# A two-layer attention trunk on one core: Q and K of four bodies as seven block products, with weight sums made by accumulating DMAs

## The chip, the core and the metric

One core of one Trainium2 chip. The metric is the device time of one execution in microseconds (us), the median of several runs. TensorE is called PE here, VectorE DVE, ScalarE ACT, GpSimd POOL and SyncE SP.

## The reference, cut to what matters

Two encoder layers over 256 tokens of width 2048, all in float32. Each layer normalizes x, multiplies it by one wide input matrix, sends slices of the result through several attention branches, gates them, multiplies by an output matrix, normalizes and adds to x.

```python
def odd_layer(x, pre_g, w_in, sink, w_out, post_g):
    h = rms_norm(x, pre_g)
    qc, kc, vc, gc, qd, kd, vd, gd = _split(h @ w_in, ODD_IN_WIDTHS)
    qc = partial_rope(qc..., pos)      # three groups of 8 heads, 128 wide
    kc = partial_rope(kc..., pos)
    oc = dilated_mixture_attention(qc, kc, vc...)   # (window, dilation) 128,1  512,4  2048,16
    ...
```

The second and third group of `dilated_mixture_attention` (dilations 4 and 16) are what the change touches: 16 heads, whose Q, K and V are 256 x 2048 times 2048 x 512 products, four heads at a time.

## The kernel before, in words

**Precision.** PE multiplies in float32r. Each weight and each activation is split into a high part (a copy rounded to float32r) and a low part (the rest), and each product is the sum of three: high x high, high x low, low x high.

**Weights.** They lie in memory as chunks of 128 x 2048 floats, 1 MB: four row blocks of 128 (a quarter of K = 2048) by 512 columns. SP loads chunk after chunk into four raw buffers (`raw`, L282), each once DVE has split what was there. ACT writes the high part of a chunk to `w_hi` (L639, `split_hi`), DVE the low part to `w_lo` (L899, `split_lo`), in three buffers each, two chunks ahead of PE. PE multiplies a chunk in two halves of 12 matmuls of 128x512 (L383, in `products`, called by `half_chunk`): 2 row blocks x 2 token tiles x 3 terms.

**Bodies.** A body is 12 chunks: four for a block of 512 columns of Q, four for K, four for V, each into its own pair of PSUM banks `acc[blk][t]`, one bank for a token tile. ACT takes a finished block out of PSUM with the norm's factor (`take`, L646) into `unit`. Layer 0 has five bodies, layer 1 eight. The first body of a layer has no attention beside it.

**Attention beside it.** While the products of body b run, the unit of body b - 1 is worked on: its Q and K are rotated by POOL (`rotate`, L334 to L341, four operations for each of Q and K), turned by PE (L463) and copied by DVE (L940), and each of four heads goes through scores (PE L481), mask and maximum (DVE L969, L980, L986), exponential (ACT L661), turning (PE L517, DVE L1024) and weighing of V (PE L529, DVE L1044). `Unit.at`, `fills` and `stages` give the half chunk (slot) at which each step stands in the order that all engines share: a body has 24 slots. At the last slot `close` merges a group's output into `mix` by its softmax weights (L1063 to L1089). Units of kind G (dilations 4 and 16) are worked on beside bodies 3 to 6 of layer 1. They turn Q and K into `postg` (`g_qT`, `g_kT`) and need no split parts, so `qT` and `kT` are idle in them. `loops` makes an instruction loop of two turns for each kind.

**Order.** Each engine runs its own instructions in the order of the text; semaphores join them. `chunk_used` counts chunks that PE is done with, `hi_ready` and `lo_ready` splits, `proj_ready` taken blocks, `roped` rotated ones. POOL issues a few DMAs, among them the two of L361 that bring x in layer 1's token order, and L364's.

## Time and profile before

| | |
|---|---|
| median of 3 runs | 1217.54 us (1216.47 to 1217.96) |
| profiled execution | 1216.43 us |
| its span | 1214.6 us |
| PE busy | 1196.7 us (99%) |
| DVE busy | 707.6 us (58%) |
| ACT busy | 562.9 us (46%) |
| POOL busy | 78.7 us (6%) |
| DMA, mean over the span | 219.90 MB, 181 GB/s |
| clock granted to PE | 0.997 |

Times of rows are microseconds from the start of the span unless ns is written. A row of a group gives the line, the engine, the operation, the tiles out<-in, the shapes and the count, then the busy time, the mean of one in ns, and the idle time of the engine just before them with what ended it. A row of the order in time gives start, duration, engine, line, operation, tiles, shapes and count, and in brackets the idle time before it.

### The profile page before, as it was taken

The page shows a single profiled execution, that of the slowest core. Times are in us where ns is not written, and L with a number is a line of the kernel's source. Part 1 is how long each engine was busy: PE and PEld are TensorE (multiplying, and loading weights), DVE is VectorE, ACT ScalarE, POOL GpSimd, SP SyncE. Part 2 cuts the span into 40 slices and gives each one's busy share as a digit, 9 for nine tenths or more (in the row PEclk, how much of TensorE's full clock was granted, in tenths as well). Part 3 has the DMA queues.
Part 4 walks back from the last instruction along what each step waited for, and adds up shares of the span by engine and source line. Part 5 has one row for each costly group of instructions (what it writes and reads, how often), then busy time and mean ns, then how long its engine had stood idle before and what let it go on. Part 6 is the DMA issues. An engine that isn't in the chain of part 4 may idle for free.

```text
span 1214.6 us, 15429 instructions
## 1 busy us (share of the span) xinstructions
PE 1196.7 (99%) x5756; PEld 1001.0 (82%) x5756; DVE 707.6 (58%) x848; ACT 562.9 (46%) x734; POOL 78.7 (6%) x129
## 2 busy tenths in 40 slices
PE   7999999999999999999999999999999999999997
PEld 5788888888888888788888888888888888888886
DVE  5375555566664955754545545565656546667554
ACT  5554343454555644564444444444344444445442
POOL 2500000300000000010000000001000001000000
PEclk9999999999999999999999999999999999999999
DMA  9995354544436454455453545454544555334541
GB/s 361 251 305 195 141 188 156 173 144 169 173 138 242 173 208 173 173 201 180 157 190 140 180 163 178 169 186 159 208 142 169 187 193 208 139 139 173 179 168 69
DMA packets 33436, 219.90 MB, mean 181 GB/s; under 512 B 4288, under 2 KB 4416, under 8 KB 7920
## 3 DMA queue, kind: packets, MB, share of 16 engines
q1 hardware_dynamic: 30672, 209.73, 48.1%
q0 software_dynamic: 1856, 7.38, 2.4%
q10 hardware_dynamic: 864, 2.18, 0.5%
q8 instruction: 31, 0.51, 0.2%
q14 instruction: 13, 0.11, 0.0%
HBM read 217.17 MB, written 2.10 MB: 181 GB/s over the span
## 4 chain that ended last, share of the span: by engine, by line
PE 95%; DMA 3%; DVE 1%; ACT 0%; SPq 0%; issue 0%; ACTq 0%; DVEq 0%
PE acc L383 85%; PE bank_x L533 2%; DMA probs<-x_nat 2%; PE bank_x L517 1%; PE bank_y L487 1%; DMA raw<-weights 1%; PE bank_x L463 1%; PE bank_y L463 1%; PE bank_y L481 1%; PE bank_x L529 1%; PE bank_y L502 0%; PE bank_x L502 0%; PE bank_x L420 0%; PE bank_y L420 0%; DVE w_lo L899 0%; ACT w_hi L639 0%
## 5 line engine op out<-in xcount | busy, mean ns | idle before, releaser
L383 PE MATMUL acc<-w_hi,act_hi 128*128 128x512 f32 x1560 | 620.7, 398 | 2.6 <-DVE w_lo L899 2.6
L383 PE MATMUL acc<-w_lo,act_hi 128*128 128x512 f32 x1560 | 609.6, 391 | 0.0
L899 DVE TENSOR_TENSOR w_lo<-raw,w_hi 128x2048 fp32r<-128x2048 f32 x195 | 448.0, 2298 | 209.0 <-ACT w_hi L639 208.8
L639 ACT ACTIVATE w_hi<-raw 128x2048 fp32r<-128x2048 f32 x195 | 373.6, 1916 | 241.2 <-PE acc L383 215.5
L383 PE MATMUL acc<-w_hi,act_lo 128*128 128x512 f32 x1560 | 418.6, 390 | 0.0
L383 PEld LDWEIGHTS acc<-w_hi,act_lo 128*128 128x128 f32 x1560 | 293.2, 188 | 62.5 <-DVE act_lo L908 0.6
L383 PEld LDWEIGHTS acc<-w_hi,act_hi 128*128 128x128 f32 x1560 | 293.6, 188 | 60.1 <-DVE w_lo L899 2.3
L383 PEld LDWEIGHTS acc<-w_lo,act_hi 128*128 128x128 f32 x1560 | 294.0, 188 | 56.5
L646 ACT ACTIVATE unit<-acc,pre_r 128x512 f32<-128x512 f32 x78 | 49.3, 684 | 114.9 <-PE acc L383 114.5
L661 ACT ACTIVATE probs<-scores,negm 128x256 f32<-128x256 f32 (+1 forms) x80 | 36.7, 459 | 127.6 <-DVE negm L986 102.3
L334 POOL TENSOR_TENSOR rope_c<-unit,cst 128x256 f32<-128x256 f32 (+1 forms) x19 | 15.1, 797 | 663.8 <-ACT unit L646 663.7
L1024 DVE COPY pT<-bank_x 128x512 f32<-128x512 f32 (+1 forms) x48 | 28.8, 600 | 48.6 <-PE bank_x L517 48.6
L1044 DVE TENSOR_SCALAR mix<-bank_x 128x256 f32 (+1 forms) x24 | 10.1, 422 | 48.1 <-PE bank_x L533 48.1
L533 PEld LDWEIGHTS bank_x<-unit,pT 128*128 128x128 f32 x256 | 33.5, 191 | 2.5
L533 PE MATMUL bank_x<-unit,pT 128*128 128x128 f32 x256 | 33.7, 274 | 0.0
L1044 DVE TENSOR_SCALAR unit_out<-bank_x 128x256 f32<-128x256 f32 x16 | 6.8, 424 | 44.4 <-PE bank_x L529 44.4
L517 PEld LDWEIGHTS bank_x<-ident,probs 128*128 128x128 f32 x160 | 20.4, 140 | 6.2
L517 PE MATMUL bank_x<-ident,probs 128*128 128x128 f32 x160 | 25.2, 272 | 0.0
L831 ACT ACTIVATE probs<-acc 128x512 f32<-128x512 f32 x16 | 9.5, 595 | 32.4 <-PE acc L383 32.4
L980 DVE TENSOR_REDUCE rmax<-scores 128x2 f32<-128x512 f32 (+1 forms) x40 | 23.2, 580 | 1.4
L1042 DVE TENSOR_TENSOR mix<-bank_x,subg 128x256 f32 x8 | 3.4, 424 | 28.6 <-ACT bank_x L712 28.6
L313 POOL DMA_DIRECT2D mix<-rpb x32 | 19.6, 683 | 0.0
(172 smaller groups left out, 619.4 us busy)
## 6 DMA issues: line engine op xcount, KB each, us to landing
raw<-weights SPq DMA_DIRECT2D x195, 1024.0 KB, 4.8
resid<-x_turned SPq DMA_DIRECT2D x8, 256.0 KB, 10.1
mix<-rpb POOLq DMA_DIRECT2D x32, 64.0 KB, 25.2
postg<-post_g POOLq DMA_DIRECT2D x2, 1024.0 KB, 24.1
resid<-x_perm POOLq DMA_DIRECT2D x2, 1024.0 KB, 8.3
out<-resid SPq DMA_DIRECT2D x8, 256.0 KB, 2.5
raw<-weights SPq DMA_DIRECT2D x2, 512.0 KB, 6.0
postg<-x_nat ACTq DMA_DIRECT2D x2, 512.0 KB, 9.6
```

The costliest lines, as they stand in the source:

```text
L313: pool.dma_start(bias_in[half * 64:half * 64 + 64, at:at + SEQ].rearrange("p (j k) -> p j k", j=ROWS), src).then_inc(bias_in_two[h // 2], 16)
L383: m = nc.tensor.matmul(tiles[t][:, :], a[:, kt, t * P:(t + 1) * P], w[:, buf, kk * NB:(kk + 1) * NB], start=(kt == 0 and a is act_hi and w ...
L463: m = nc.tensor.transpose(bank[f % 2][:, n * P:(n + 1) * P], unit[:, blk, t, h * HEAD:(h + 1) * HEAD], ident[:, :])
L517: m = nc.tensor.transpose(X[:, at:at + P], p[:, t * w + k * P:t * w + (k + 1) * P], ident[:, :])
L533: m = nc.tensor.matmul(X[:, t * P:(t + 1) * P], pT[:, k * SEQ + t * P:k * SEQ + (t + 1) * P], unit[:, 2, k, col:col + HEAD], start=(k == 0 ...
L639: nc.scalar.activation(w_hi[:, at % SPLIT, :], raw[:, at % RAW, :], ACT.Copy).then_inc(S["hi_ready"], 1)
L646: m = nc.scalar.activation(dst[:, t, :], acc[blk][t][:, :], ACT.Copy, scale=pre_r[:, t:t + 1])
L661: m = nc.scalar.activation(probs[:, j % 2, t * w:(t + 1) * w], scores[:, j % 2, t * w:(t + 1) * w], ACT.Exp, bias=negm[:, 2 * j + t:2 * j ...
L899: nc.vector.tensor_tensor(w_lo[:, at % SPLIT, :], raw[:, at % RAW, :], w_hi[:, at % SPLIT, :].bitcast(F32), ALU.subtract).then_inc(S["lo_r ...
L980: nc.vector.reduce_max(rmax[:, two], dst.rearrange("p (t n) -> p t n", t=NT), AX_X).then_inc(S["maxed"], 1)
L1024: nc.vector.tensor_copy(pT[:, 0:n], X[:, 0:n]).then_inc(S["pt_ready"], 1)
L1044: nc.vector.tensor_scalar(dst, src, 1.0, None, ALU.mult).then_inc(S["o_taken"], 1)
```

## The change

In bodies 3 to 6 of layer 1, Q and K are no longer computed as eight products of (a token tile) x (half of K) by (half of K) x (the columns of Q or of K). With A11, A12 (first token tile; first, second half of K), A21, A22 (second tile), W11, W21 (columns of Q; first, second half of K), W12, W22 (columns of K), there are seven products (after Strassen and Winograd). They are named by their weight operand: W11 with A11; W21 with A12; P = W11 + W12 with S1; Q = W11 + W12 + W22 (as the source names it: P's block plus the next) with S2; R = W22 + W12 with S3; T = the sum of all four with A22; W22 with S5. S1, S2, S3 and S5 are sums and differences of parts of A, made once, in layer 1's first body (`sums`), and split into high and low.

- The body's list is `FAST_OPS`: 18 operations, each one chunk of 128x2048. V has four with 24 matmuls; the other fourteen have 12 matmuls each, into one bank of 128 tokens. A V operation has two slots, the others one: 22 slots.
- The sums of weights are made in the raw buffers: POOL issues a DMA of a further chunk with `accum_op=ALU.add` onto the chunk that is there, once DVE has split it: eight per body, behind POOL's two rotations. SP issues ten plain loads per body, in a written order, with a fifth raw buffer (`spare`, in the idle halves of `qT` and `kT`).
- ACT and DVE split most chunks in halves (`fast_split`), with semaphores for halves, and PE waits for high and low parts of each half on their own.
- ACT takes two results, DVE combines the rest out of PSUM: five `scalar_tensor_tensor` of 128x512. K is ready before Q, and POOL rotates in that order.
- x of layer 1 is kept in memory (`x_kept`) as `resid` holds sums; it comes back after the last G rotation. The loops over G bodies are written out.

```diff
+FAST0, FAST = 3, 4
+FAST_OPS = (("W11", 0), ("W11", 1), ("V", 0), ("V", 1), ("P", 0), ("P", 1), ("W21", 0), ("W22", 0), ("W22", 1),
+            ("Q", 0), ("Q", 1), ("V", 2), ("R", 0), ("R", 1), ("W21", 1), ("T", 0), ("T", 1), ("V", 3))
+FAST_RAW = (0, 1, 2, 3, 0, 1, 4, 2, 3, 0, 1, 4, 2, 3, 4, 0, 1, 2)
+FAST_SLOTS = [(o, x) for o, (name, _) in enumerate(FAST_OPS) for x in ((0, 1) if name == "V" else (None,))]
...
 @block.sync
+            for k in range(FAST):
+                op, d = first_op(1, FAST0 + k), CHUNK0[1] + BODY * (FAST0 + k)
+                load(2, d + 6, op + 3)
+                load(3, d + 7, op + 4)
+                load(4, d + 10, op + 7)
+                load(4, d + 3, op + 12)
+                load(2, d + 11, op + 13)
+                d += BODY
+                if k < FAST - 1:
+                    load(3, d + 9, op + 14)
+                    load(4, d + 2, op + 15)
+                    load(0, d, op + 16)
+                    load(1, d + 1, op + 17)
+                    load(2, d + 8, op + 18)
...
 @block.gpsimd
                     for k, (blk, cols) in enumerate(turns):
                         pool.wait_ge(S["proj_ready"], PROJ0[layer] + 3 * u.body - 2 + k)
                         pool.wait_ge(S["roped"], CREDIT + 2 * (u.index - 2) + k)
                         rotate(u, k, blk, cols, HEAD // 2 if layer == 0 else HEAD)
+                    if u.kind == "G":
+                        op, d = first_op(1, u.body), CHUNK0[1] + BODY * u.body
+                        for o, chunk in ((4, 4), (5, 5), (9, 6), (10, 7), (12, 4), (13, 5), (15, 2), (16, 3)):
+                            r = FAST_RAW[o]
+                            before = max(n for n in range(o) if FAST_RAW[n] == r)
+                            pool.wait_ge(S["lo_ready"], op + before + 1)
+                            pool.dma_start(raw[:, r, :], weights[d + chunk], accum_op=ALU.add).then_inc(added[r], 16)
...
 @block.tensor
+            def fast_body(u):
+                for h, (o, part) in enumerate(FAST_SLOTS):
+                    attention(u, h)
+                    name, c = FAST_OPS[o]
+                    ...
+                    if o == 6:
+                        pe.wait_ge(S["n1_taken"], k + 1)
+                    if o == 7:
+                        pe.wait_ge(S["n5_taken"], k + 1)
+                    if o == 12:
+                        pe.wait_ge(S["n6_taken"], k + 1)
+                    if o == 15:
+                        pe.wait_ge(S["proj_ready"], proj + 1)
+                    for half in (0, 1) if part is None else (part,):
+                        ... # wait for this half's high part; per row block: high and low of A times it
+                        ... # wait for this half's low part; per row block: high of A times it
+                        m.then_inc(S["chunk_used" if half else "half_used"], 1)
...
 @block.scalar
+            def fast_split(u, h):
+                k, op = u.body - FAST0, first_op(1, u.body)
+                o, part = FAST_SLOTS[h]
+                n = o + 2
+                ... # n >= FAST_N: whole split of the next body's chunk 0 or 1
+                for half in (0, 1) if part is None else (part,):
+                    if half == 0:
+                        if FAST_OPS[n][0] in FAST_SUMS:
+                            act.wait_ge(added[FAST_RAW[n]], fast_sums(k, n))
+                        else:
+                            act.wait_ge(landed[FAST_RAW[n]], fast_landings(k, n))
+                    if half == 0 and n >= 3:
+                        act.wait_ge(S["half_used"], FAST_N * k + n - 2)
+                    else:
+                        act.wait_ge(S["chunk_used"], op + n - 2)
+                    nc.scalar.activation(w_hi[:, buf, half * 2 * NB:(half + 1) * 2 * NB], raw_part(FAST_RAW[n], half),
+                                         ACT.Copy).then_inc(S["hi_ready" if half else "hi_half"], 1)
...
 @block.vector, fast_body: at each slot, ahead of attention(u, h) and fast_split(u, h)
+                    if h == 8:
+                        dve.wait_ge(S["chunk_used"], op + 6)
+                        ...
+                        nc.vector.scalar_tensor_tensor(c22, sum_c[:, :], r[1], c21, ALU.mult, ALU.subtract).then_inc(
+                            S["n5_taken"], 1)
+                    if h == 13:  # c12 from sum_b, n6_taken
+                    if h == 14:  # c12 from sum_c
+                    if h == 17:  # c22 from sum_b, proj_ready (K)
+                    if h == 20:  # c21 from sum_b, proj_ready (Q)
+            def sums(s):  # layer 1's first body, slots 6 to 11: 8 sums, 4 low parts, 128x1024 each
```

## Rows read from the trace of the kernel before

**Rows 1.** The page: engines over the span, and the chain by engine and line.
```profile
PE 1196.7 (99%) x5756; PEld 1001.0 (82%) x5756; DVE 707.6 (58%) x848; ACT 562.9 (46%) x734; POOL 78.7 (6%) x129
PE 95%; DMA 3%; DVE 1%; ACT 0%; SPq 0%; issue 0%; ACTq 0%; DVEq 0%
```
**Rows 2.** The chain in order of time, around 800 us: start, us, what.
```profile
800.49 5.47 PE acc L383 x24
...
809.59 0.45 PE bank_y L481 x4
810.04 8.18 PE acc L383 x36
...
821.18 0.44 PE bank_x L529 x4
```
**Rows 3.** ACT in order of time: the take of V, once in each body.
```profile
722.42 1.27 ACT L646 ACTIVATE unit<-acc,pre_r 128x512 f32<-128x512 f32 x2 [3.52 <-PE acc L383]
794.21 1.27 ACT L646 ACTIVATE unit<-acc,pre_r 128x512 f32<-128x512 f32 x2 [3.42 <-PE acc L383]
865.96 1.27 ACT L646 ACTIVATE unit<-acc,pre_r 128x512 f32<-128x512 f32 x2 [3.42 <-PE acc L383]
937.72 1.27 ACT L646 ACTIVATE unit<-acc,pre_r 128x512 f32<-128x512 f32 x2 [3.42 <-PE acc L383]
1009.53 0.69 ACT L646 ACTIVATE unit<-acc,pre_r 128x512 f32<-128x512 f32 x1 [3.48 <-PE acc L383]
```
**Rows 4.** Busy time by stretch, about a body each: length, engines, clock, DMA share, GB/s.
```profile
791.00:863.00 72.00, 72.00 (x346) 60.20 (x346) 42.13 (x55) 30.09 (x35) 4.60 (x8) 1.00 0.48 175
863.00:935.00 72.00, 72.00 (x346) 60.20 (x346) 42.12 (x54) 30.09 (x35) 4.60 (x8) 1.00 0.51 178
```
**Rows 5.** DVE in order of time in a G body, and groups of the whole span.
```profile
786.37 2.28 DVE L899 TENSOR_TENSOR w_lo<-raw,w_hi 128x2048 fp32r<-128x2048 f32 x1
788.57 0.16 DVE L1063 TENSOR_TENSOR newneg<-cneg,negm 128x8 f32<-128x8 f32 x1
...
797.31 2.29 DVE L899 TENSOR_TENSOR w_lo<-raw,w_hi 128x2048 fp32r<-128x2048 f32 x1 [0.22 <-ACT w_hi L639]
...
L894 DVE TENSOR_TENSOR w_lo<-raw,w_hi 128x1024 fp32r<-128x1024 f32 x2 | 2.5, 1226 | 3.2 <-ACT w_hi L631 1.9 <-ACT w_hi L628 1.3
L940 DVE COPY postg<-bank_x 128x512 f32<-128x512 f32 x8 | 5.5, 692 | 12.1 <-PE bank_x L463 12.1
L1024 DVE COPY pT<-bank_x 128x256 f32<-128x256 f32 x16 | 6.8, 424 | 22.7 <-PE bank_x L517 22.7
```
**Rows 6.** ACT by groups: splits of a whole chunk and of a half.
```profile
L639 ACT ACTIVATE w_hi<-raw 128x2048 fp32r<-128x2048 f32 x195 | 373.6, 1916 | 241.2 <-PE acc L383 215.5 <-DMA raw<-weights 25.6
L628 ACT ACTIVATE w_hi<-raw 128x1024 fp32r<-128x1024 f32 x1 | 1.1, 1056 | 1.1 <-DMA raw<-weights 1.1
```
**Rows 7.** POOL and DVE in order of time, at two rotations.
```profile
534.23 0.73 POOL L334 TENSOR_TENSOR rope_c<-unit,cst 128x256 f32<-128x256 f32 x1 [161.87 <-ACT unit L646]
535.88 2.29 DVE L899 TENSOR_TENSOR w_lo<-raw,w_hi 128x2048 fp32r<-128x2048 f32 x1 [3.14 <-ACT w_hi L639]
535.88 2.89 POOL L341 TENSOR_TENSOR unit<-rope_c,rope_s 128x256 f32<-128x256 f32 x1
...
1010.06 2.28 DVE L899 TENSOR_TENSOR w_lo<-raw,w_hi 128x2048 fp32r<-128x2048 f32 x1
1010.87 1.79 POOL L334 TENSOR_TENSOR rope_c<-unit,cst 128x128 f32<-128x128 f32 x1 [21.31 <-ACT unit L646]
1012.91 2.36 POOL L337 TENSOR_TENSOR rope_s<-unit,cst 128x64 f32<-128x64 f32 x1
```
**Rows 8.** DMA: a stretch with its engines full; issues by line; one of POOL's alone.
```profile
800.00:804.00 4.00, 4.00 (x22) 3.36 (x21) 3.58 (x3) 1.57 (x1) 0.00 (x0) 1.00 0.98 406
raw<-weights SPq DMA_DIRECT2D x195, 1024.0 KB, 4.8
mix<-rpb POOLq DMA_DIRECT2D x32, 64.0 KB, 25.2
postg<-post_g POOLq DMA_DIRECT2D x2, 1024.0 KB, 24.1
resid<-x_perm POOLq DMA_DIRECT2D x2, 1024.0 KB, 8.3
L364 POOL DMA_DIRECT2D postg<-post_g x1 | 0.6, 591 | 0.0
DMA to landing us min/median/max: 6.8/6.8/6.8
```

More of the change, by code:

```diff
@@ L229, in build @@
         x_new = [sem(f"x_new{t}") for t in range(NT)]
-        landed = [sem(f"landed{i}") for i in range(RAW)]
+        landed = [sem(f"landed{i}") for i in range(RAW + 1)]
+        added = [sem(f"added{i}") for i in range(RAW)]
         bias_in_two = [sem(f"bias_in_two{i}") for i in range(UH)]
@@ L244, in loops @@
                     yield Unit(kind, lay, body, index, 0, mask), body, 0
+                elif kind == "G" or eng is nc.gpsimd and lay == 1:
+                    for i in range(count):
+                        yield Unit(kind, lay, body, index, i, mask), body, i
                 else:
@@ L275, in _, with ring @@
                 load_x(2 * c + 1)
-            with sp.Fori(1, ALL_CHUNKS // RAW) as n:
-                src = [sp.snap(n * RAW + r) for r in range(RAW)]
-                free = [sp.snap(n * RAW + r - RAW + 1) for r in range(RAW)]
-                for r in range(RAW):
-                    sp.wait_ge(S["lo_ready"], free[r])
-                    sp.dma_start(raw[:, r, :], weights[bass.ds(src[r], 1)].rearrange("a p n -> p (a n)")).then_inc(
-                        landed[r], 16)
+            def ring(first, rounds, chunk, op):
+                with sp.Fori(first, first + rounds) as n:
+                    src = [sp.snap(n * RAW + r + chunk) for r in range(RAW)]
+                    free = [sp.snap(n * RAW + r + op - RAW + 1) for r in range(RAW)]
+                    for r in range(RAW):
+                        sp.wait_ge(S["lo_ready"], free[r])
+                        sp.dma_start(raw[:, r, :], weights[bass.ds(src[r], 1)].rearrange("a p n -> p (a n)")).then_inc(
+                            landed[r], 16)
@@ new lines, in load @@
+            def load(r, chunk, used):
+                sp.wait_ge(S["lo_ready"], used)
+                if r < RAW:
+                    sp.dma_start(raw[:, r, :], weights[chunk]).then_inc(landed[r], 16)
+                else:
+                    for half in range(2):
+                        sp.dma_start(spare[half], weights[chunk][:, half * 2 * NB:(half + 1) * 2 * NB]).then_inc(
+                            landed[r], 16)
+            ring(1, RING - 1, 0, 0)
+            op, d = first_op(1, FAST0), CHUNK0[1] + BODY * FAST0
@@ new lines, in _ @@
+            load(0, d, op - 3)
+            load(1, d + 1, op - 2)
+            load(2, d + 8, op - 1)
+            load(3, d + 9, op)
+            sp.wait_ge(S["masked"], 4 * UH)
+            load(4, d + 2, op)
+            for k in range(FAST):
[13 more added lines that the diff above has]
+                else:
+                    for r in range(RAW):
+                        load(r, d + r, (op + 16, op + 17, op + 18, op + 14)[r])
@@ L350, in _ @@
                     turns = ((0, NB), (1, NB), (2, 2 * HEAD)) if u.kind == "D" else ((0, NB), (1, NB))
+                    if layer == 1 and u.body > FAST0:
+                        turns = ((1, NB), (0, NB)) + turns[2:]
                     for k, (blk, cols) in enumerate(turns):
@@ L557, in _ @@
                 for u, b, i in loops(pe, layer):
+                    if u is not None and u.kind == "G":
+                        fast_body(u)
+                        continue
                     for h in range(2 * BODY):
@@ new lines, in fast_body @@
+            def fast_body(u):
+                k, op = u.body - FAST0, first_op(1, u.body)
+                for h in range(len(FAST_SLOTS)):
+                    if h == 0:
+                        act.wait_ge(S["o_full"], u.head(0))
+                        take(op, 2, unit[:, 2, :, :])
+                    if h == 3:
+                        act.wait_ge(S["chunk_used"], op + 2)
+                        act.wait_ge(S["qk_full"], 4 * u.index + 2)
+                        for t in range(NT):
+                            m = nc.scalar.activation(unit[:, 0, t, :], sum_a[:, :], ACT.Copy, scale=pre_r[:, t:t + 1])
+                        m.then_inc(S["n1_taken"], 1)
+                    if h == 18:
+                        act.wait_ge(S["chunk_used"], op + 15)
+                        act.wait_ge(S["n6_taken"], k + 1)
+                        nc.scalar.activation(unit[:, 0, 0, :], sum_a[:, :], ACT.Copy, scale=pre_r[:, 0:1]).then_inc(
+                            S["c11_taken"], 1)
+                    attention(u, h)
+                    fast_split(u, h)
@@ L787, in _ @@
                 for u, b, i in loops(act, layer):
+                    if u is not None and u.kind == "G":
+                        fast_body(u)
+                        continue
                     for s in range(BODY):
@@ L819, in _ @@
                             pre_squares(layer, s - 3)
+                        if u is None and layer == 1:
+                            sums(s)
                         if u is None and s == 4:
@@ L1191, in _ @@
                 for u, b, i in loops(dve, layer):
+                    if u is not None and u.kind == "G":
+                        fast_body(u)
+                        continue
                     for s in range(BODY):
```

238 lines of the change are left out of this document (217 added, 21 removed).

## The prediction

> **What bounds the kernel now.** I read the page's engine table and its chain first [rows 1]. TensorE is busy for 99% of the span, 95% of the chain is PE, and 85% is the one line that multiplies weight blocks into `acc`; what PE waits for adds up to a few microseconds. The chain in order of time shows how such a stretch is built [rows 2]: 24 products of 128x512 (one chunk of 1 MB of weights: 4 row blocks, 2 token tiles, 3 terms) take 5.47 us, 36 take 8.18, so one product costs 0.227 us and a half chunk 2.72. Attention puts in pieces of 0.44 us between them. The take of V by ScalarE marks the start of a body [rows 3]: 722.42, 794.21, 865.96, 937.72, 1009.53, so each of the four bodies that the change touches (bodies 3 to 6 of layer 1, the G units) lasts 71.77 us. Of this 12 x 5.45 = 65.4 are weight products and 6.4 attention. In them DVE is busy 42.1 us, ACT 30.1, POOL 4.6, and the DMA engines 48 to 51% at 175 to 178 GB/s [rows 4]. PE alone sets the time. The other engines have slack, and the change spends it.
>
> **What is removed.** Eight block products of 24 matmuls (2 token tiles x 2 halves of K x the Q and K columns) become seven. The V product stays at 96 matmuls, Q and K go from 192 to 168: 264 in place of 288 in a body. 24 x 0.227 = 5.45 us per body, **21.8 us** over four. No attention matmul is removed. If PE stays the bound, a body lasts 71.77 - 5.45 = 66.3 us. Whole products are counted at their present pace because a satisfied wait at a chunk border costs no visible time: 36 products across borders take 8.18 us, exactly 3 x 2.73 [rows 2]. So the new waits on halves cost nothing where the data is there.
>
> **What is added on DVE.** Twelve weight chunks per body are split into high and low parts now, eighteen afterwards, because a summed block feeds one bank instead of two. A whole split has a pitch of 2.20 us (786.37 to 788.57) [rows 5]. Sixteen of the eighteen are done in halves. A half lasts 1.226 us [rows 5], and I take its pitch as 1.13, less the same overlap of 0.09. That is 2 x 2.20 + 16 x 2.26 = 40.6 us. The rest of DVE's body is 42.1 - 12 x 2.29 = 14.6. Five combining operations of 128x512 out of PSUM at 0.62 (row 0.69 less the overlap) add 3.1. Total 58.3 of 66.3 us, 88% where it was 59%. The tightest stretch is the seven one-bank operations P0 to Q1. PE needs 7 x 2.72 + 1.2 of attention = 20.2 us; DVE needs 7 x 2.26, one combination at 0.69, two copies at 0.42 and one head's output, mask, maximum and negation, all of 128x256 or less, about 1.5 together, in all 18.8 [rows 5]. It fits, by 1.4 us, and the splits run two operations ahead, so DVE may lag by 2.7 us before PE stands. Cost on the path: between 0 and, if every hand-over slips, 4 us a body. I take 0.7, **3 us** in all, nearer to nothing, as PE's idle in the present bodies is nothing while DVE does the same chain of copies.
>
> **On ACT**: 2 x 1.92 + 16 x 2 x 1.06 [rows 6] + 7.1 of other work that is there now + nothing more for taking (five pieces in place of six) = 45 of 66.3 us. Hidden. **Sums of activations**: twelve DVE operations and four ScalarE copies of 128x1024 in layer 1's first body, 1.23 and 1.06 us each [rows 5, 6]. The fullest slot has three of 1.23 and a split of 2.29 = 6.0 us against PE's 5.45, followed by a slot with 3.5. Hidden; 0, at most 1 us. Keeping x in memory and bringing it back are 4 MB of transfers with tens of microseconds of room: 0. SP's loads keep an order in which every wait is due before the next one; unrolling is 0.
>
> **Added on POOL and DMA, the disputed cost.** POOL's queue now has, in each body, behind the two rotations, eight accumulating loads of 1 MB, each waiting until the block's old contents are split. Issue is 0.59 us each [rows 8], 4.7 us, harmless. What such a transfer costs, no row shows. Plain loads move 406 GB/s while the engines are full [rows 8]: 1.049 MB is 2.6 us of all 16 engines, 4.8 us from issue to landing, and from POOL 6.8, or 8.3 for two together [rows 8]. Lower end: an accumulating load costs as much as a plain one. Then a body moves 18 blocks, 47 us of 66.3, and PE stays the bound. Upper end: POOL's rows of 24.1 and 25.2 us to landing [rows 8]. Taken as one transfer at a time that would be 8 x 24 = 193 us a body, +485 us in all; they stood in a full queue at the start, so this is only a far end. In between, call the cost r plain loads. Engines full all the time give (10 + 8r) x 2.6; with 5% lost in hand-overs of buffers (an estimate) the body is that over 0.95. PE stays the bound up to (66.3 x 0.95 / 2.6 - 10) / 8 = 1.78; the gain is gone at (71.77 x 0.95 / 2.6 - 10) / 8 = 2.03. I take a value between 1 and 1.75, as the nearest rows are plain loads of the same size and queue.
>
> The margins in time, at such a cost: the block for P0 is asked for after the second rotation and has until PE reaches operation 4, 16 us into the body, less 2 us of splitting; R0 is free 2.5 us into the slot of operation 5 and is wanted by ACT at the slot of operation 10, five slots of 2.72 less 2.5, and some attention, 12 us. Against 7 to 9 us to landing all hold.
>
> *First rule weighed.* The second rotation stands ahead of P0's load, and it isn't always short. Its first operation takes 0.73 undisturbed, and the last, of the same shape, 2.89 where a DVE split begins at the same moment (535.88); two operations on a half and a quarter of the elements take 1.79 and 2.36 at 1010.87 and 1012.91, where DVE splits again [rows 7]. With DVE at 88% each of the four can meet a split or a merge: up to 4 x 1.8 = 7 us more. At r below 1.75 that still lands by 12 us into the body, before PE wants it at 16. At r of 2 it costs 2 us a body. The Trainium skill (SBUF — State Buffer, Who interferes with whom) has it that a DVE instruction with two SBUF inputs blocks a GpSimd one that reads SBUF; the trace agrees, with the 2.89 for 0.73.
>
> **Rivals.**
> (a) *DMA engines at about twice the price of a plain load (r 1.75 to 2.1)*: an accumulate reads two streams, weights and old contents, and writes one. At r = 2 the engines need 26 x 2.6 = 67.6 us, over 0.95 = 71.2; with 1 us for the rotation 72.2, so +0.4 x 4 = +2: **1219**, between -8 and +12. For: the rate of 406 GB/s looks like a ceiling on one stream. Against: the page's engines are busy only half of the time, and the old contents come from SBUF, not from memory.
> The Trainium skill (Collectives: The Full Stack, The bandwidth ceiling: the fold count and why AG ≠ RS ≠ AR) says that an adding transfer issues two reads per chunk and measures a ratio of 1.93. By that the sum would be (10 + 8 x 1.93) x 2.6 / 0.95 = 69.6 us a body, 1209. No run here shows it yet.
> (b) *The transfers become the bound outright (r above 2.1), slower than before.* It decides from r = 2.03. Place: PE waits at P, Q, R and T for their high part. Price at 2.4: 29.2 x 2.6 / 0.95 = 79.9, +8.1 a body, +33: **1250**; at 3, 93.1, +85: 1303. For: no accumulating transfer is in the trace, and SP's plain loads for V and W queue on the same engines. Against: nothing in the rows.
> (c) *DVE paces the body*: 58.3 us of work and some fifty hand-overs. At the 0.22 us that DVE stands between ACT's end and its own start in a dense place [rows 5] it reaches 69.3, and only 2.5 a body are gained: **1208**. Against: where DVE's data lies ready its operations follow each other without a gap.
>
> **How the numbers follow.** The profiled execution had a span of 1214.6 and lasted 1216.43, 1.8 around the span, and lies 1.1 under the median of 1217.54. On its own time: 1216.4 - 21.8 + 3 = 1197.6; on the median's, **1199**. Chances: this forecast 0.42, (a) 0.24, (b) 0.27, (c) 0.07. Faster by over 0.2% (2.4 us, about what a measurement can tell): 0.42 + 0.06 + 0.09 of (a) = 0.57. Same: 0.06. Slower: 0.27 + 0.10 of (a) = 0.37. The forecast's own range is 1194 to 1204. The full range goes from 1194 to 1250: below is left 0.03, above the dearer half of (b), 0.14.
>
> **What would show it.** Right: the V takes of the fast bodies 66 to 67 us apart; PE still without idle in its products of weights; DMA busy 70 to 85% in these bodies; time to landing of accumulating loads under 10 us; DVE near 58 us a body. Wrong towards (a) and (b): DMA busy above 93%, ACT's high part waiting for a DMA on `raw`, landing above 10 us, bodies of 71 us and more. Wrong towards (c): PE waiting for `w_lo` while DMA has idle. The sum would be wrong too if PE's pitch left 0.227 us, or if its clock, granted in full now [rows 4], fell in new waits.

## The result, and the profile after

The changed kernel takes **1230.28 us** (median of 4 runs, 1228.88 to 1233.93) against 1217.75 for the kernel before, measured beside it: ratio 1.0108 [1.0082, 1.0134]. It is slower by 12.5 us, where 1199 was forecast. The kernel before was measured again beside each later run, with medians from 1216.4 to 1216.6; so two variants are compared below by their distances from it, and 1 us more or less is not read. The profiled execution lasted 1233.93 us, its span is 1231.9.

The page of the changed kernel answers to [rows 1] and [rows 8]: busy time of each engine, DMA queues (packets, MB, share of 16 engines), the chain by engine and line, and DMA issues with KB and median us to landing.

```profile
PE 1187.1 (96%) x5660; PEld 989.0 (80%) x5660; DVE 794.7 (65%) x969; ACT 613.6 (50%) x822; POOL 114.7 (9%) x165
...
q1 hardware_dynamic: 31248, 201.34, 45.3%
q0 software_dynamic: 7040, 45.13, 16.6%
...
PE 73%; DMA 15%; DVE 6%; ACT 3%; issue 2%; POOL 1%; SPq 0%; DVEq 0%; ACTq 0%
...
raw<-weights POOLq DMA_DIRECT2D x32, 1024.0 KB, 12.2
g_turned<-weights SPq DMA_DIRECT2D x24, 512.0 KB, 10.1
```

PE has 96 matmuls fewer, as the change says, and was on 95% of the chain and is on 73%. DMA went from 3% to 15%. The accumulating loads (POOL's 32) take 12.2 us to landing. The halves of 0.5 MB that SP loads into the fifth buffer, which the page calls `g_turned`, take 10.1 although they are half as large.

ACT in order of time, the take of V once in each fast body, answers to [rows 3] (columns as there):

```profile
721.90 1.27 ACT L848 ACTIVATE unit<-acc,pre_r 128x512 f32<-128x512 f32 x2 [3.58 <-PE acc L517]
796.08 1.27 ACT L848 ACTIVATE unit<-acc,pre_r 128x512 f32<-128x512 f32 x2
873.64 1.27 ACT L848 ACTIVATE unit<-acc,pre_r 128x512 f32<-128x512 f32 x2
...
1027.24 1.27 ACT L848 ACTIVATE unit<-acc,pre_r 128x512 f32<-128x512 f32 x2
```

The take of the first body stands where it stood, within 0.5 us: nothing was lost ahead of the fast bodies. Then the spacing is 74.2, 77.6, 77.8 and 75.8 us instead of 71.8 (the take left out between the last two rows starts at 951.47). The window over one of these bodies (from a Q rotation to the next) answers to [rows 4] (length; busy time of PE, PEld, DVE, ACT, POOL; granted clock, DMA share, GB/s):

```profile
791.40:868.90 77.50, 69.91 (x322) 57.47 (x321) 60.05 (x81) 42.62 (x57) 14.49 (x16) 0.96 0.89 244
```

PE idles 7.6 of the 77.5 us, nearly all in two places, of 3.57 us ahead of 838.60 and of 3.85 ahead of 854.78. PE in order of time at the second:

```profile
854.78 1.22 PE L663 MATMUL bank_x<-unit,pT 128*128 128x128 f32 x4 [3.85 <-DVE pT L1297]
```

The releaser named is a small DVE copy of attention, which is not the cause: it stood in DVE's order behind a split, and that split behind a load. The chain of waits tells it (start, us, what):

```profile
792.20 0.72 POOL rope_c L453
792.92 2.46 POOL rope_s L454
...
796.61 0.52 POOL raw L485
797.14 13.42 DMA raw<-weights
...
818.24 0.33 SPq L372
818.61 16.14 DMA g_turned<-weights
834.77 1.06 ACT w_hi L999
...
838.24 0.33 SPq L372
838.61 12.31 DMA g_turned<-weights
850.95 1.06 ACT w_hi L999
...
854.39 0.34 DVE pT L1297
854.78 1.22 PE bank_x L663 x4
```

Three transfers take 41.9 us of one body's chain: P0's accumulating load behind the second rotation, and two loads into the fifth buffer, whose rows are 4 KB because each is a half. Over these bodies ACT waits 44.8 us for `g_turned` in 7 waits and 21.3 us for `raw` in 9. And PE's clock fell after the second wait. Windows of 3 us, columns as above:

```profile
851.00:854.00 3.00, 0.00 (x0) 0.00 (x0) 1.97 (x2) 3.00 (x4) 0.00 (x0) 0.99 0.93 393
854.00:857.00 3.00, 2.22 (x9) 2.21 (x10) 3.00 (x5) 2.73 (x3) 0.00 (x0) 0.50 0.53 152
```

After an idle of 3.85 us the granted clock is 0.50, the 1.2 GHz level, for some 7 us. The wait of 3.57 us before it was followed by a clock of 1.00, and a wait of 2.46 us in the next body (until 915.45) by 0.57 over the next 3 us: the length of the wait alone does not decide it. So the body is 66.8 us of work (the next section measures that) + 7.6 of waits + 3.1 of slower matmuls (69.91 busy less 66.8) = 77.5.

### The profile page after: what moved, and what is told of

Same layout as the page of the kernel before. It is cut to its first block, busy times and chain, and to the rows that moved or that the text cites. A ratio compares the mean times of both kernels' runs of the same rounds, so it can differ in the third digit from the quotient of the medians.

```text
span 1231.9 us, 15094 instructions
## 1 busy us (share of the span) xinstructions
PE 1187.1 (96%) x5660; PEld 989.0 (80%) x5660; DVE 794.7 (65%) x969; ACT 613.6 (50%) x822; POOL 114.7 (9%) x165
## 4 chain that ended last, share of the span: by engine, by line
PE 73%; DMA 15%; DVE 6%; ACT 3%; issue 2%; POOL 1%; SPq 0%; DVEq 0%; ACTq 0%
PE acc L517 61%; DMA g_turned<-weights 8%; DMA raw<-weights 7%; DVE w_lo L1472 3%; PE bank_x L667 2%; PE acc L724 2%; ACT w_hi L999 1%; PE bank_y L621 1%; PE bank_x L651 1%; PE acc L735 1%; DVE w_lo L1172 1%; ACT w_hi L841 1%; ACT w_hi L987 1%; PE bank_x L597 1%; PE bank_y L597 1%
## 5 line engine op out<-in xcount | busy, mean ns | idle before, releaser
L517 PE MATMUL acc<-w_hi,act_hi 128*128 128x512 f32 x1176 | 466.2, 396 | 4.0 <-DVE w_lo L1172 4.0
L517 PE MATMUL acc<-w_lo,act_hi 128*128 128x512 f32 x1176 | 459.0, 390 | 0.0
L1172 DVE TENSOR_TENSOR w_lo<-raw,w_hi 128x2048 fp32r<-128x2048 f32 x147 | 337.8, 2298 | 161.8 <-ACT w_hi L841 161.5
L841 ACT ACTIVATE w_hi<-raw 128x2048 fp32r<-128x2048 f32 x147 | 281.7, 1916 | 155.7 <-PE acc L517 133.6
L517 PEld LDWEIGHTS acc<-w_hi,act_hi 128*128 128x128 f32 x1176 | 221.1, 188 | 48.3 <-DVE w_lo L1172 4.3
L517 PEld LDWEIGHTS acc<-w_hi,act_lo 128*128 128x128 f32 x1176 | 220.6, 188 | 47.0 <-DVE act_lo L1190 0.3
L517 PEld LDWEIGHTS acc<-w_lo,act_hi 128*128 128x128 f32 x1176 | 221.2, 188 | 43.1
L1472 DVE TENSOR_TENSOR w_lo<-raw,w_hi 128x1024 fp32r<-128x1024 f32 x104 | 125.1, 1240 | 15.5 <-ACT w_hi L999 15.2
L999 ACT ACTIVATE w_hi<-raw 128x1024 fp32r<-128x1024 f32 x104 | 104.8, 1051 | 29.7 <-DMA raw<-weights 21.3
L724 PE MATMUL acc<-w_hi,act_hi 128*128 128x512 f32 x224 | 83.4, 419 | 0.0
L848 ACT ACTIVATE unit<-acc,pre_r 128x512 f32<-128x512 f32 x62 | 39.2, 684 | 71.8 <-PE acc L517 71.3
L735 PE MATMUL acc<-w_lo,act_hi 128*128 128x512 f32 x224 | 65.2, 396 | 0.0
L1472 DVE TENSOR_TENSOR w_lo<-g_turned,w_hi 128x1024 fp32r<-128x1024 f32 x24 | 28.3, 1222 | 45.8 <-ACT w_hi L999 45.8
L724 PEld LDWEIGHTS acc<-w_hi,act_lo 128*128 128x128 f32 x224 | 44.1, 197 | 9.3
L735 PEld LDWEIGHTS acc<-w_lo,act_hi 128*128 128x128 f32 x224 | 43.4, 194 | 9.6
L724 PEld LDWEIGHTS acc<-w_hi,act_hi 128*128 128x128 f32 x224 | 42.5, 198 | 7.5
L999 ACT ACTIVATE w_hi<-g_turned 128x1024 fp32r<-128x1024 f32 x24 | 24.1, 1049 | 45.2 <-DMA g_turned<-weights 44.8
## 6 DMA issues: line engine op xcount, KB each, us to landing
raw<-weights POOLq DMA_DIRECT2D x32, 1024.0 KB, 12.2
g_turned<-weights SPq DMA_DIRECT2D x24, 512.0 KB, 10.1
```

The source lines that it names most:

```text
L517: m = nc.tensor.matmul(tiles[t][:, :], a[:, kt, t * P:(t + 1) * P], w[:, buf, kk * NB:(kk + 1) * NB], start=(kt == 0 and a is act_hi and w ...
L724: m = nc.tensor.matmul(fast_bank(name, t)[:, :], fast_left(name, c, kk, t)[n], w_hi[:, buf, kk * NB:(kk + 1) * NB], start=(name in ("W11", ...
L735: m = nc.tensor.matmul(fast_bank(name, t)[:, :], fast_left(name, c, kk, t)[0], w_lo[:, buf, kk * NB:(kk + 1) * NB], start=False, stop=(kk ...
L841: nc.scalar.activation(w_hi[:, at % SPLIT, :], raw[:, at % RAW, :], ACT.Copy).then_inc(S["hi_ready"], 1)
L848: m = nc.scalar.activation(dst[:, t, :], acc[blk][t][:, :], ACT.Copy, scale=pre_r[:, t:t + 1])
L999: nc.scalar.activation(w_hi[:, buf, half * 2 * NB:(half + 1) * 2 * NB], raw_part(FAST_RAW[n], half), ACT.Copy).then_inc(S["hi_ready" if ha ...
```

## The experiments

The expectations number their theories. Theory 1, **price**: an accumulating load costs about two plain ones, and the DMA engines are full. Theory 2, **order**: P0's load stands behind the second rotation, and loads follow each other into the one fifth buffer. Theory 3, **DVE**: its 60 us a body pace everything. Theory 4, **turns**: beyond its price, the queues are served packet by packet, so a transfer with short rows (small packets) falls behind one with long rows. Theory 5, **clock**: the half clock makes the waits dearer.

**Eight plain loads in place of the accumulating ones.**

```diff
-pool.dma_start(raw[:, r, :], weights[d + chunk], accum_op=ALU.add).then_inc(added[r], 16)
+pool.dma_start(raw[:, r, :], weights[d + chunk]).then_inc(added[r], 16)
```

> The eight accumulating loads of a fast body become plain loads of the same chunks by the same queue (the sums of weights are left out, so P, Q, R and T multiply single chunks). Theory 1, the price of an accumulating load on the DMA engines: with 18 plain loads the engines are needed for 47 to 50 us of a body, V takes come 66 to 68 us apart, PE has no wait and no stretch at half clock, time 1197 to 1204. Theory 2, the order (P0's load behind Q's rotation, two loads in a row into the one spare buffer): the waits stay, bodies of 72 to 75 us, time 1217 to 1226. Theory 3, DVE and its hand-overs: bodies stay near 77, time about 1230.

Measured: **1194.59** us (1193.97 to 1196.34), ratio 0.9824 [0.9807, 0.9840], 21.9 us under the 1216.47 beside it, and a little under theory 1's range. The window over a body, columns as above:

```profile
783.00:850.00 67.00, 66.84 (x323) 55.53 (x321) 60.75 (x82) 43.54 (x57) 11.84 (x16) 1.00 0.77 284
```

PE has no idle, with DVE busy 60.8 of 67 us. It leaves out the sums of weights, so its result is not the layer's, but the same bytes, waits, splits, combinations and order of POOL are in it. So everything lost comes with the one argument, and theory 3 is refuted. The order and the half rows cost nothing either where all loads are plain. The mean body is 66.8 us.

**Half of them plain**: P and Q accumulate, R and T do not (their sums are left out).

```diff
+**({"accum_op": ALU.add} if o < 12 else {})
```

> Only the loads for R and T are plain (four of eight; the sums R and T are left out), P and Q accumulate. Theory 1: the engines need 10 x 2.7 + 4 x 2.7 + 4 x 5.1 = 58 us of a body, under the 66 that PE needs: within 3 us of the kernel with eight plain loads, 1197 to 1206. Theory 2: the wait at V2 and W21 stays where P's and Q's loads stand before it: 1213 to 1220. Theory 3: about 1230.

Measured: **1197.79** (1196.13 to 1200.73), ratio 0.9841 [0.9825, 0.9858], inside theory 1's range. Four accumulating loads a body cost 3.2 us in all, eight cost 34.4 (12.5 above the kernel before, where none gives 21.9 below): the loss is not so much for each load, it starts where the engines run out.

**The price by itself.** A kernel of transfers only, run once, 1 MB each: from memory to SBUF sixteen plain ones of SP, sixteen accumulating ones from POOL with four in flight, four plain and four accumulating ones one at a time, sixteen plain, sixteen accumulating beside plain ones of SP, then 4 MB within memory.

```
for n in range(16):
    b = n % 4
    if n >= 4:
        pool.wait_ge(added[b], 16 * (n // 4))
    pool.dma_start(buf[b][:, :], weights[n], accum_op=ALU.add).then_inc(added[b], 16)
```

> No computation: only transfers of 1 MB chunks, in stretches: 16 plain loads from SP with four in flight, 16 accumulating ones from POOL with four in flight, four plain and four accumulating ones one at a time, 16 plain ones from POOL, 16 accumulating ones beside 16 of SP's, then 4 MB copied and 4 MB accumulated within memory. Theory 1: plain 2.6 us each from either queue, accumulating 5.0 to 5.3 us each with four in flight, and beside SP's the sum of both. If an accumulating load were cheap on the engines and only slow to land (theory 2), four in flight would move at 3 us each and a single one would take 8 us or more.

Measured, POOL in order of time: first and last issue of each series once four are in flight (12 issues in each series, 11 for the last), and between them one of the accumulating loads that go one at a time (L64):

```profile
51.98 0.86 POOL L56 DMA_DIRECT2D b<-weights  x1 [4.78 <-DMA b<-weights]
...
106.07 0.86 POOL L56 DMA_DIRECT2D b<-weights  x1 [4.03 <-DMA b<-weights]
...
163.88 0.86 POOL L64 DMA_DIRECT2D b<-weights  x1 [7.56 <-DMA b<-weights]
...
185.59 0.53 POOL L71 DMA_DIRECT2D b<-weights  x1 [3.21 <-DMA b<-weights]
...
212.90 0.53 POOL L71 DMA_DIRECT2D b<-weights  x1 [1.95 <-DMA b<-weights]
...
244.49 0.86 POOL L79 DMA_DIRECT2D b<-weights  x1 [6.62 <-DMA b<-weights]
...
318.70 0.87 POOL L79 DMA_DIRECT2D b<-weights  x1 [6.61 <-DMA b<-weights]
```

Accumulating (L56): 54.09 / 11 = **4.92 us**. Plain (L71): 27.31 / 11 = **2.48 us**. The ratio r is **1.98**. Beside a stream of plain loads (L79) the pitch is 74.21 / 10 = 7.42 us, which is 4.92 + 2.48: the two share the same engines and nothing overlaps. One at a time, an accumulating load has a period of 8.2 to 8.4 us (L64, 7.56 of wait and 0.86 of issue), a plain one 5.3. The Trainium skill (Collectives: The Full Stack, The bandwidth ceiling: the fold count and why AG ≠ RS ≠ AR) has a measured ratio of 1.93 between a copying and an adding collective, and puts it down to two source reads. The ratio agrees with the 1.98 here; that the second read is the reason here too is not shown by any run.

By that price the engines need 10 x 2.48 + 8 x 4.92 = 64.2 us a body, just under PE's 66.8. It alone does not give 77.

**Row sizes.** In a second kernel of transfers only, run once, SP loads 1 MB, whole (8 KB rows) or as two halves (4 KB rows), alone and beside the accumulating stream.

```
for h in range(2):
    sp.dma_start(buf[4][:, h * 1024:(h + 1) * 1024], weights[n][:, h * 1024:(h + 1) * 1024]).then_inc(halves, 16)
sp.wait_ge(halves, 32 * (n + 5))
```

> No computation. SP loads 1 MB at a time into one buffer, four times as rows of 8 KB and four times as two transfers with rows of 4 KB: first alone, then beside a steady stream of accumulating loads from POOL. Theory 4, an engine gives each queue one packet in turn, whatever its size: alone both take 4.5 to 5 us; beside the stream 8 packets of 8 KB each wait for one accumulating packet (0.61 us): 8 x (0.31 + 0.61) + 2 = 9.4 us, and 16 packets of 4 KB: 16 x (0.16 + 0.61) + 2 = 14.3 us. Rival, the bytes are shared and not the packets: both forms take 9 to 10 us.

The four lines of SP's loads; L29 is whole alone, L33 halves alone, L39 and L43 the same beside the stream:

```profile
L29 SPq DMA_DIRECT2D b<-weights x4: 327/328/328, 13.0 to 27.4; - x4
DMA to landing us min/median/max: 4.7/4.8/4.9
...
L33 SPq DMA_DIRECT2D b<-weights x8: 328/380/433, 32.2 to 47.9; - x8
DMA to landing us min/median/max: 3.8/4.3/4.8
...
L39 SPq DMA_DIRECT2D b<-weights x4: 328/328/328, 61.4 to 95.8; - x4
DMA to landing us min/median/max: 11.1/11.4/11.7
...
L43 SPq DMA_DIRECT2D b<-weights x8: 327/394/506, 107.1 to 155.8; - x8
DMA to landing us min/median/max: 9.7/13.0/16.2
```

Alone, rows of 4 or 8 KB make hardly a difference to 1 MB (4.8 us whole, 3.8 and 4.8 for the halves, each from its own issue). Beside the stream the whole load takes 11.4 us and the halves 16.2 at most, a difference of 4.8 where the turns gave 4.9 (14.3 less 9.4) and sharing by bytes gave none. Both are 2 us longer than the turns gave, which stays open. In terms of turns, the same megabyte has twice the packets, and each waits for an accumulating one of full length. The 16.14 us of the chain is of this size.

**The fifth buffer in one piece**, so that one transfer of 8 KB rows fills it.

```diff
-g_qT, g_kT = g_turned[:, 0, :], g_turned[:, 2, :]
-spare = [g_turned[:, 1, :], g_turned[:, 3, :]]
+g_qT, g_kT = g_turned[:, 0, :], g_turned[:, 1, :]
+spare = [g_turned[:, 2, :], g_turned[:, 3, :]]
...
-for half in range(2):
-    sp.dma_start(spare[half], weights[chunk][:, half * 2 * NB:(half + 1) * 2 * NB]).then_inc(landed[r], 16)
+sp.dma_start(g_turned[:, 2:4, :].rearrange("p a n -> p (a n)"), weights[chunk]).then_inc(landed[r], 16)
```

> As the changed kernel, but the fifth raw buffer lies in one piece, so its three loads per body are one transfer of 8 KB rows in place of two of 4 KB rows; the turned Q and K take the first two quarters. Theory 4: these loads land 5 to 6 us earlier where they run beside accumulating ones, the two waits of PE (3.6 and 3.9 us in body 4) and the half clock behind the second shrink: 4 to 7 us a body, 1205 to 1215. Theory 1 alone (the engines have no room at all): the accumulating loads then land later by as much, no change, 1226 to 1230.

Measured: **1217.74** (1215.55 to 1221.12), ratio 1.0012 [1.0000, 1.0023]: 11.2 of the 12.5 us lost against the kernel before are gone by the shape of twelve loads. That is far under theory 1 alone (1226 to 1230) and above theory 4's 1205 to 1215. A body's window, its two DMA queues from 788 to 862 us (packets, MB, share of 16 engines), and the longest piece of the chain over it:

```profile
788.50:862.50 74.00, 69.61 (x320) 57.40 (x320) 60.57 (x81) 42.50 (x56) 14.58 (x16) 0.96 0.92 256
```

```profile
q0 software_dynamic: 1152, 8.39, 56.7%
q1 hardware_dynamic: 1438, 10.48, 35.1%
...
830.88 11.57 DMA g_turned<-weights
```

The load into the fifth buffer takes 11.57 us where it took 16.14. The accumulating queue's eight loads took 56.7% of 16 engines' time and the plain queue's ten 35.1%, so 5.2 and 2.6 us a load, 68 of 74 us. In the kernel both kinds cost some 5% more than by themselves, and why is not shown; but with it the engines alone need more than PE's 66.8. They are 92% full: the price of the loads sets the length of the body.

**P0's load ahead of the second rotation.**

```diff
+if u.kind == "G" and k == 1:
+    add_chunk(4, 4)
 rotate(u, k, blk, cols, ...)
-for o, chunk in ((4, 4), (5, 5), (9, 6), ...):
+for o, chunk in ((5, 5), (9, 6), ...):
```

> As the changed kernel, but POOL issues P0's accumulating load ahead of Q's rotation, as soon as the chunk there is split. Theory 1: the engines are at 89% of the body as it is; the six microseconds in which they stand idle while POOL waits and rotates shrink by about half: 2 to 3 us a body in three bodies, time 1221 to 1226. Theory 2: the chain starts some 7 us earlier in each of three bodies: 1208 to 1213. Theory 3: no change, 1230.

Measured: **1227.78** (1225.30 to 1228.40), ratio 1.0088 [1.0071, 1.0105]: 11.3 us above the kernel before, for the changed kernel's 12.5, and the intervals overlap. The rotation delays the load by 4.4 us (792.20 to 796.6, with a 2.46 for an operation of 0.46), and in the chain that stood ahead of the 13.42. At most 0.6 us a body comes back, less than theories 1 and 2 gave it, and it is not clear of the noise.

**Both edits.**

> The spare buffer in one piece and P0's load ahead of Q's rotation. Theory 4 with theory 2: the engines' own need is 10 x 2.48 + 8 x 4.92 = 64.2 us of a body, PE's 66.8: 67 to 70 us a body, 1197 to 1208. Theory 1 alone: as the kernel with the early P0 load, 1225 to 1228.

Measured: **1216.33** (1214.48 to 1219.34), ratio 0.9996 [0.9986, 1.0006]. That is 1.4 under the fifth buffer alone, with overlapping intervals, and misses both forecasts. The 1197 to 1208 rested on a need of 64.2 us of engine time a body, by the prices measured by themselves; in the kernel it is 68, as the version above shows. So order and shape are spent, and only fewer engine microseconds are left.

**Accumulating loads in rows of 4 KB** (with the fifth buffer whole), to give the plain loads more turns.

```diff
-accum_op=ALU.add).then_inc(added[r], 16)
+accum_op=ALU.add, max_dma_last_dim=4096).then_inc(added[r], 16)
```

> The spare buffer in one piece, and the eight accumulating loads go in rows of 4 KB in place of 8 KB. The bytes and sums are the same. Theory 4: SP's plain loads get half of an engine's time beside them in place of a third; the spare loads land at about 7 us (10.7 before), the accumulating ones no later in total, 2 to 5 us less a body: 1203 to 1212. Theory 1 (the price of accumulating is per byte and fills the engines): no change, 1215 to 1220; and if each row costs a fixed time, slower.

Measured: **1232.36** (1230.47 to 1233.57), ratio 1.0132 [1.0115, 1.0149], some 14.5 us slower than without, where theory 4 forecast a gain. The waits of PE (us in total, times, longest) moved:

```profile
PE acc L724 <- ACT w_hi L999: 11.3, 3, 3.9
PE acc L724 <- DVE unit L1502: 7.2, 4, 2.8
```

The loads into the fifth buffer landed sooner (median 9.8 us for 10.7), the longest accumulating one took 27.8 us where it had been 21.8 (medians 11.3 and 11.4), and ACT waited 84.9 us for `raw`, 40.5 before. That is as turns would have it: with full engines a turn given to one queue is taken from the other, and here the sums were the later. But the accumulating queue also took 59.0% of the engines for the same 8.39 MB, 1.7 us a body more or about 7 us in all (an estimate), and no run separates the two.

**Half clock: PE kept busy** by 14 extra matmuls at slots 13 and 17 of each fast body, in the changed kernel.

```diff
+if h in (13, 17):
+    for n in range(14):
+        nc.tensor.matmul(acc[1][1][:, :], act_hi[:, 0, 0:P], ..., start=True, stop=True)
```

> As the changed kernel, with 14 more matmuls of 128x512 into a bank that nobody reads, 3.2 us, ahead of the steps of attention at the slots 13 and 17 of each fast body, where PE waits 2.5 to 5.2 us. Theory 5, half of the loss behind a wait is PE's granted clock of 0.50 for the 7 us after it: with PE kept busy the clock stays full, 2 to 3 us less in each body, 1219 to 1224. Rival, the slow stretch costs nothing since the transfers are the bound anyway: 1229 to 1233.

Measured: **1228.17** (1224.84 to 1229.55), ratio 1.0085 [1.0067, 1.0103]. The window over the fast bodies:

```profile
720.00:1020.00 300.00, 292.56 (x1390) 241.35 (x1389) 232.34 (x306) 166.77 (x223) 54.18 (x62) 1.00 0.90 244
```

The changed kernel has PE busy 274.34 us at 0.95 in the same window. Here the clock is full throughout, and no wait of PE is over 2.2 us. The kernel lies 11.6 us above the one before, the changed kernel 12.5, and the intervals overlap: between the two forecasts, and close to the rival's. In the window of a body PE was busy 73.5 of 77.5 us, so the extra matmuls themselves had room. So the slow matmuls are a result of the waits and hardly a cause of the time: the transfers set the pace at either clock.

**Sums made in memory beforehand.** If accumulation costs engine time, it can be spent where the engines are half idle [rows 4]. P = W11 + W12 and R = W22 + W12 of the four bodies are built in memory while layer 0 runs, and loaded plain. Q and T still accumulate onto them. Four accumulating loads a body are left, as in the second experiment.

```diff
+pool.dma_start(summed[at:at + 2], weights[d + chunk:d + chunk + 2]).then_inc(S["pre_copied"], 16)   # x8
+pool.wait_ge(S["pre_copied"], 16 * 2 * FAST)
+pool.dma_start(summed[at:at + 2], weights[d + 4:d + 6], accum_op=ALU.add, max_dma_last_dim=8192)   # x8
... # the loops around the transfers, and a semaphore for the sums, are left out
+if FAST_OPS[o][0] in ("P", "R"):
+    pool.dma_start(raw[:, r, :], summed[4 * (u.body - FAST0) + chunk]).then_inc(added[r], 16)
```

> P and R of all four bodies are summed in memory beforehand, while layer 0 runs (16 MB copied, 16 MB accumulated on top, by POOL's queue), and the fast bodies load them plainly; only Q and T accumulate onto the buffers, four loads in place of eight. The whole result is computed. Spare buffer in one piece. The engines' need in a fast body is 14 x 2.48 + 4 x 4.92 = 54.4 us of 66.8. Theory 1: bodies of 67 us, 1196 to 1201, if layer 0 hides the 131 us of transfers in its idle half. If it doesn't (its weight loads wait behind accumulating packets), layer 0 gets longer by 10 us or more: 1206 and up.

Measured: **1249.33** (1248.50 to 1251.81), ratio 1.0277 [1.0260, 1.0294]. The fast bodies are down to 67.9, 68.2 and 68.9 us, as hoped, but layer 0 lost some 46 us. A window of it, and DMA queues and issues from 82 to 138 us:

```profile
80.00:140.00 60.00, 33.50 (x151) 27.27 (x150) 16.70 (x19) 13.12 (x16) 3.93 (x8) 0.81 1.00 361
```

```profile
q0 software_dynamic: 404, 16.91, 82.5%
...
raw<-weights SPq DMA_DIRECT2D x4, 1024.0 KB, 40.1
```

The copies go in packets of 42 KB on average (16.91 MB in 404), and a weight load of 8 KB rows takes 40.1 us beside them, part of it behind the weight loads issued before it. That looks like the turns at their worst; the next run tests it.

**The same with rows of 2 KB in memory**, for the copies and for the accumulating transfers.

```diff
-pool.dma_start(summed[at:at + 2], weights[d + chunk:d + chunk + 2])
+pool.dma_start(summed[at:at + 2], weights[d + chunk:d + chunk + 2], max_dma_last_dim=2048)
...
-pool.dma_start(summed[at:at + 2], weights[d + 4:d + 6], accum_op=ALU.add, max_dma_last_dim=8192)
+pool.dma_start(summed[at:at + 2], weights[d + 4:d + 6], accum_op=ALU.add, max_dma_last_dim=2048)
```

> As the kernel with P and R summed in memory beforehand, but those transfers within memory go in rows of 2 KB (before: the copies in rows of 64 KB, the accumulating ones of 8 KB). The whole result is computed. Theory 4, one packet of each queue in turn: SP's 8 KB packets now wait 0.1 to 0.2 us each in place of 0.6 to 3 us; the 46 us that layer 0 lost come back but for 0 to 5, and the fast bodies stay at 68 us: 1202 to 1209. Rival, the engines' total load in layer 0 is what delayed it: 1240 or more.

Measured: **1245.87** (1244.23 to 1250.12), ratio 1.0235 [1.0218, 1.0252]. During the copies PE is now busy 60.0 of 60 us at 390 GB/s, and a weight load lands after 11.2 us (below, from 82 to 138 us), so the long packets were the cause there. But the time hardly moved. It lies in the range of the rival, that the engines' whole load delays layer 0, and yet not by that: PE has one wait that accounts for it, and POOL's waits around it say why (us, times, longest):

```profile
raw<-weights SPq DMA_DIRECT2D x8, 1024.0 KB, 11.2
...
POOL summed L474 <- issue: 94.0, 1, 94.0
...
PE bank_x L616 <- POOL unit L459: 45.4, 1, 45.4
```

**The transfers moved in POOL's order**: those of the first two bodies behind layer 0's last rotation, the others behind the residual's loads.

```diff
 if layer == 0:
+    pool.wait_ge(S["pre_copied"], 16 * 2 * FAST)
+    add_in_memory((0, 1))
     pool.wait_ge(S["map1_full"], 2 * UH)
     for t in range(NT):
         pool.dma_start(resid[:, t, :], x_perm[t * P:(t + 1) * P, :]).then_inc(S["resid_in"], 16)
+    add_in_memory((2, 3))
```

> The run with 2 KB rows in the memory transfers, with its eight accumulating transfers in memory issued elsewhere on POOL: those for the first two fast bodies behind layer 0's last rotation, those for the other two behind the residual's loads, none ahead of a rotation. In that run POOL's eighth such issue lasted until 274.2 us (94.0 us of issue), the rotation of unit stood behind it, and PE waited for that rotation once, for 45.4 us. If the loss of layer 0 was POOL's queue, and not traffic, it goes whole: the profiled 1248.3 us less 45 gives 1203 (1200 to 1208), about 14 us under the kernel before, fast bodies 68 us as there, and no PE wait over 5 us between 140 and 720 us. The rival is that 2 MB accumulating transfers in memory disturb the weight loads wherever they lie: then the weight loads of 340 to 500 us land beyond 16 us, PE waits some 10 to 25 us there, and the time is 1215 to 1228, no better than before.

Measured: **1202.94** (1200.94 to 1204.71), ratio **0.9884 [0.9868, 0.9901]**: 13.5 us faster than the kernel before, with all seven products and sums computed, and some 26 faster than the changed kernel. It is the time forecast, 1203, so the loss of the run before was POOL's queue. Its page, and a window where the memory transfers run:

```profile
PE 1179.1 (98%) x5660; PEld 982.8 (82%) x5660; DVE 793.8 (66%) x969; ACT 616.2 (51%) x822; POOL 126.7 (11%) x181
...
summed<-weights POOLq DMA_DIRECT2D x16, 2048.0 KB, 47.7
raw<-summed POOLq DMA_DIRECT2D x16, 1024.0 KB, 6.5
raw<-weights POOLq DMA_DIRECT2D x16, 1024.0 KB, 8.7
```

```profile
340.00:440.00 100.00, 100.00 (x490) 84.03 (x490) 69.89 (x108) 52.90 (x82) 6.52 (x6) 1.00 0.96 279
```

The engines are 96% full there and PE loses nothing. It moves 34 MB more than the changed kernel and is faster: bytes count only where their queue is full.

## Why the prediction was wrong

**The step that failed** is the choice of r. The prediction bounded it from 1 upwards, named 1.78 as where PE stops being the bound and 2.03 as where the gain is gone, and then took "a value between 1 and 1.75, as the nearest rows are plain loads of the same size and queue". It measured 1.98. With r = 1 the rest of the sum held: plain loads in the same places gave 1194.6. Nearness in size and queue said nothing about a transfer that must also take in the old contents of the buffer. Rival (a) named the engines at twice the price, at 0.24. The 1.93 of the Trainium skill (Collectives: The Full Stack, the section named above), against the measured 1.98, was the better evidence, though the prediction's sum with it, 1209, still lies 9 us under the version that has this mechanism alone (1217.74).

**The second failure** is that no case held the changed kernel's own loss. Rival (a) at r = 2 gave 72.2 us a body and 1219. The version with the fifth buffer in one piece has the same mechanism and measured 1217.74, with 72.6 us a body by the takes of V. The changed kernel lies some 11 above it because the prediction counted all 18 blocks as equal, the fifth buffer's three in halves among them. So 1230 is (a) plus what the half rows cost, and the turns are the theory that fits it; rival (b), r above 2.1, is refuted by the 1.98 although its 1250 lay on the right side.

Point by point:
- *Removed, 21.8 us*: right. With plain loads the kernel is 21.9 us under the one before, and the bodies are 66.8 us for 66.3.
- *DVE, 58.3 us and up to 3 us of stalls*: 60.8 measured, and no stall (PE idle 0.2 of 67 us). The 3 us were not needed, rival (c) is out.
- *ACT 45 us, sums of activations, keeping x, SP's order*: hidden, as said. ACT 42 to 43.5; the first V take is not later; the plain-load run leaves room for none of them.
- *Issue 0.59 us each*: 0.86 for an accumulating one; harmless too.
- *Margins, "Against 7 to 9 us to landing all hold"*: landing was 7.6 to 19.5, median 12.2, for a margin of 12 at R0. They did not hold.
- *The rotation ahead of P0's load, 2 us a body at r of 2* (the sum of (a) takes 1): it was on the chain, but moving the load returned at most 0.6 a body. The stretched operation is there (2.46 us).
- *Hand-over loss 5% of the engines*: 8% in the body shown of the version with the whole buffer, 68 of 74 us, and about 6% of the mean 72.6. The 68 are (a)'s 67.6.
- *Signs*: V takes at 71 and more, ACT waiting for `raw`, landing over 10 us pointed to (a), as listed. "DMA busy above 93%" came in the first fast body only (94, 89, 91 and 83% over the four): the engines stood still while the loads waited for the rotation (share 0.00 from 794 to 798 us), so some 90% was already the bound. The fall of PE's clock was listed as a danger; it came, and filling the waits returned about 1 us in all.

## What to carry to other kernels

Before a matmul is traded for a transfer, price the transfer in microseconds of all 16 DMA engines, in a kernel of its own: an accumulating load counted 2.0 plain ones, and the traded kernel gained 22 us, gained 19 or lost 12 (1 with long rows everywhere) according to whether none, four or eight of eighteen loads in a body were of that kind. Leave a margin: in the kernel the loads took 5% more than by themselves, and 6 to 8% went in hand-overs. Near a full set of engines, try all transfers on the critical ring with the same long rows first. Move accumulation to a stretch where the engines are half idle and behind whatever POOL's in-order queue owes to others; that made the same idea 13.5 us faster than before.

## What the runs showed of the hardware that was not expected

- What a load loses beside another queue goes by the number and size of packets, as if queues took turns by packet: 1 MB in 8 KB rows lands after 4.8 us alone, 11.4 beside an accumulating stream of 8 KB rows, 40.1 beside memory copies in packets of some 42 KB (with weight loads before it in its queue) and 11.2 beside them in 2 KB rows; in 4 KB rows 16.2 beside the accumulating stream.
- The prices add without overlap: 4.92 + 2.48 = 7.40 against 7.42 measured when both kinds run. The rate is 424 GB/s plain and 214 accumulating with the engines full.
- After a wait of 3.85 us PE's clock was at 0.50 for some 7 us, after one of 3.57 us it stayed at 1.00; in the run whose longest wait was 2.2 us it stayed at 1.00 throughout.
- POOL stood 94.0 us at a DMA issue, without a semaphore, when seven transfers of 2 MB in 2 KB rows stood before it; in the last run, with three before it, the fourth stood 5.1 us. What limits it was not tried.
